# A mixture-of-experts layer whose last stage is folded into the expert blocks: the second expert's block adds the first one's row, normalises and writes the output

## The reference

```python
h = rmsnorm(x, norm_pre_ffn) * (1.0 + sc2) + sh2         # x: stream after token mixing
grp = argmax(h @ w_rg + b_rg)                            # 1 group of 4
top_v, top_i = lax.top_k(le_sel, 2)                      # 2 experts of the 8 of that group
w_top = softmax(top_v) * gate_g
def expert_block(args):                                  # 128 rows of one expert
    hid = silu(xb @ w_gate[e]) * (xb @ w_up[e])          # 1024 -> 512
    return hid @ w_down[e]                               # 512 -> 1024
out = sum over the two experts of a token of w_top * its row
x = x + g2 * rmsnorm(out, norm_post_ffn)                 # the result
```

## Time and profile before

| | us |
|---|---|
| runs | 2747.73, 2748.4, 2756.85 (median 2748.4) |
| span of the profiled execution | 2748.3 |
| own time of the profiled execution | not listed apart from its span |
| expert blocks, from the first instruction to PE's end | 1713 to 2640.9 |
| from the end of the last expert product to the end of the span | 107.4 |
| granted TensorE clock, mean | 0.924 of full speed |

### The profile page before, as it was taken

One profiled execution on the slowest core, in us unless ns is written; L12 is line 12 of the kernel. 1 busy time (PEld: TensorE's weight loads), 2 busy tenths in 40 slices (PEclk: granted clock), 3 DMA queues, 4 the chain that ended last, 5 costly groups with the idle time before them and its releaser, 6 DMA issues. The chain is left out here.

```text
span 2748.3 us, 36137 instructions
## 1 busy us (share of the span) xinstructions
PE 2291.0 (83%) x11720; PEld 1881.1 (68%) x11721; DVE 1460.6 (53%) x1901; ACT 1063.1 (39%) x1517; POOL 671.3 (24%) x743
## 2 busy tenths in 40 slices
PE   5899998999995626888867995799999999999940
PEld 2688887989983225666656884577777777787730
DVE  2333331111104865887864775286576656538857
ACT  2433333322221211433322222276566655537731
POOL 0000000000003345777731223222122212112322
PEclk8899999999996879999988996899999999999975
DMA  7222233121215868534435331498588868558968
GB/s 253 86 92 92 92 108 115 47 93 46 90 52 193 317 216 300 207 141 153 153 95 198 146 133 52 138 323 299 200 305 282 283 216 279 205 181 308 368 240 320
DMA packets 294684, 509.46 MB, mean 185 GB/s; under 512 B 35104, under 2 KB 209600, under 8 KB 290368
## 3 DMA queue, kind: packets, MB, share of 16 engines
q1 hardware_dynamic: 261200, 403.20, 42.4%
q0 software_dynamic: 21904, 63.54, 6.6%
q10 hardware_dynamic: 11520, 41.95, 3.8%
HBM read 408.16 MB, written 110.43 MB: 189 GB/s over the span
## 5 line engine op out<-in xcount | busy, mean ns | idle before, releaser
L2146 DVE TENSOR_TENSOR e_w_low<-e_w_whole,e_w_high 128x2048 fp32r<-128x2048 f32 x192 | 432.2, 2292 | 82.9 <-ACT e_w_high L2102 82.6
L2102 ACT ACTIVATE e_w_high<-e_w_whole 128x2048 fp32r<-128x2048 f32 x192 | 356.5, 1909 | 17.9 <-PEq L1491 12.3
L2056 PE MATMUL e_pG<-e_w_high,e_xT 128*128 128x512 f32 x768 | 305.0, 397 | 1.2 <-ACT e_xT L2095 1.2
L2057 PE MATMUL e_pG<-e_w_low,e_xT 128*128 128x512 f32 x768 | 305.3, 397 | 0.0
L611 PE MATMUL proj_acc<-w_high,hT_high 128*128 128x512 f32 x672 | 265.6, 395 | 6.9 <-DVE hT_low L646 5.7
L611 PE MATMUL proj_acc<-w_low,hT_high 128*128 128x512 f32 x672 | 263.0, 391 | 0.0
L611 PE MATMUL proj_acc<-w_high,hT_low 128*128 128x512 f32 x672 | 262.8, 391 | 0.0
L2075 PE MATMUL e_pY<-e_w_high,e_hT 128*128 128x512 f32 x768 | 221.7, 400 | 0.0
L2060 PE MATMUL e_pG<-e_w_high,e_xT 128*128 128x512 f32 x768 | 194.9, 395 | 0.0
L307 POOL TENSOR_TENSOR stat<-stat,eps 128x1 f32<-128x1 f32 x36 | 10.8, 300 | 725.0 <-ACT xn L515 725.0
L2056 PEld LDWEIGHTS e_pG<-e_w_high,e_xT 128*128 128x128 f32 x768 | 145.2, 189 | 36.6 <-issue 1.6
(11 more groups left out here) (287 smaller groups left out, 4403.3 us busy)
## 6 DMA issues: line engine op xcount, KB each, us to landing
e_w_whole<-in_moe_w_gate_dram SPq DMA_DIRECT2D x64, 1024.0 KB, 7.6
e_w_whole<-in_moe_w_up_dram SPq DMA_DIRECT2D x64, 1024.0 KB, 10.9
e_w_whole<-in_moe_w_down_dram SPq DMA_DIRECT2D x64, 1024.0 KB, 9.3
m_tok<-by_token SPq DMA_DIRECT2D x16, 1280.0 KB, 6.9
xt<-in_x_dram SPq DMA_DIRECT2D x32, 512.0 KB, 5.4
wm_rest<-in_w_mod_dram POOLq DMA_DIRECT2D x8, 2048.0 KB, 12.2
c_yy<-rows_done SPq DMA_DIRECT2D x32, 512.0 KB, 7.4
by_token<-tok SPq DMA_DIRECT2D x16, 768.0 KB, 5.6
```

The costliest lines, as they stand in the source:

```text
L2056: nc.tensor.matmul(pG[:, half], xT[:, 0, k], wh[:, half, w], start=(k == 0), stop=False)
L2057: nc.tensor.matmul(pG[:, half], xT[:, 0, k], wl[:, half, w], start=False, stop=False)
L2102: nc.scalar.activation(wh[:, third, part], raw[:, third, part], ACT.Copy).then_inc(whs.sem, 1)
L2146: nc.vector.tensor_tensor(wl[:, third, part], raw[:, third, part], wh[:, third, part].bitcast(F32), ALU.subtract).then_inc(wls.sem, 1)
```

## The change

There is no `combine`. The list entry of a row has five numbers in place of two: the token to gather; the row of a scratch tensor (now 2048 rows) if this expert is the token's first, that with the smaller number, or else a number out of range; the same token number if it is the second, or else out of range; the weight; and 1.0 or 0.0 for second or not. Out-of-range rows are skipped by the DMAs, padding rows too. In a block, DVE multiplies the hidden rows by the weight (as a scalar of the same instruction), then, at the end, adds the partner's row times the flag to the product (one instruction over 1024 columns from PSUM); ACT squares the sum; POOL scatters it to the first rows, makes the inverse root, and gathers the partner rows of the next block after that scatter has landed; DVE scales by the root and the modulation; in the next round POOL adds the residual rows, which it has gathered, scatters them to the output, and DVE hands the row numbers on through four small tiles. In `projection` POOL copies the input `x`, 8 MB, into the scratch tensor halfway, so that a skipped or stale row holds finite numbers.

```diff
@@ projection, POOL
-            with pool.Fori(0, 2 * NGR) as t:
...
+            roots(0, NGR)
+            pool.dma_start(dram["ys"], io["x"].rearrange("o t d -> (o t) d")).then_inc(ys_init.sem(0), 16)
+            roots(NGR, 2 * NGR)
+            pool.wait_ge(ys_init.sem(0), ys_init.at(0))
@@ residual, DVE: choose and place
+                V.tensor_tensor(fl[:, s, 0:1], fe[:, 0:1], fe[:, 1:2], ALU.is_lt)
+                link(V.tensor_tensor(fl[:, s, 1:2], fe[:, 1:2], fe[:, 0:1], ALU.is_lt))
...
-                link(V.reciprocal(g["wtop"][:, 0, r:r + 1], dn[:]))
-                link(V.tensor_tensor(g["wtop"][:, 1, r:r + 1], g["wtop"][:, 0, r:r + 1], ex[:, s], ALU.mult))
+                w0, w1 = (token[:, r, k, 3:4].bitcast(F32) for k in range(2))
+                link(V.reciprocal(w0, dn[:]))
+                link(V.tensor_tensor(w1, w0, ex[:, s], ALU.mult))
+                for k in range(2):
+                    V.scalar_tensor_tensor(out=to[:, k, 0:1], in0=fl[:, s, 1 - k:2 - k], scalar=float(SKIP), in1=row_f[:, r:r + 1], op0=ALU.mult, op1=ALU.add)
+                    m = V.scalar_tensor_tensor(out=to[:, k, 1:2], in0=fl[:, s, k:k + 1], scalar=float(SKIP), in1=row_f[:, r:r + 1], op0=ALU.mult, op1=ALU.add)
+                link(m)
+                link(V.tensor_copy(token[:, r, :, 1:3], to[:]))
+                for k in range(2):
+                    m = V.tensor_copy(token[:, r, k, 4:5].bitcast(F32), fl[:, s, 1 - k:2 - k])
+                link(m)
@@ experts, POOL
+            for at in (ids, held, first, second, done_row):
+                nc.gpsimd.memset(at[:], SKIP).then_inc(none.sem, 1)
+            for t in (xb[:], v[:], z, partner[:], x1):
+                nc.gpsimd.memset(t, 0.0).then_inc(none.sem, 1)
...
+            def load_ids(b, row):
+                pool.wait_ge(held_on.sem, held_on.at(b - 1))
+                pool.dma_start(ids[:], dram["ids"][bass.ds(row, P), :]).then_inc(ids_in.sem(0), 16)
+            def complete(b):
+                pool.wait_ge(x1_in.sem(0), b * 16 + 16)
+                pool.wait_ge(zs.sem, zs.at(b - 3))
+                nc.gpsimd.tensor_tensor(z, z, x1, ALU.add).then_inc(done.sem, 1)
+                pool.wait_ge(done.sem, done.at(b))
+                pool.indirect_dma_start(out_rows, rows(done_row, 0), z, None, bounds_check=SEQ - 1, oob_is_err=False).then_inc(out.sem(0), 16)
+            def gather_x1():
+                pool.indirect_dma_start(x1, None, x1_rows, rows(second, 0), ...).then_inc(x1_in.sem(0), 16)
+            def root(b):
+                pool.wait_ge(ssq.sem, ssq.at(b - 2))
+                nc.gpsimd.tensor_tensor(ss[:, 1:2], ss[:, 0:1], g["eps"][...], ALU.add).then_inc(eps_added.sem, 1)
+                nc.gpsimd.tensor_tensor(ss[:, 1:2], ss[:, 1:2], g["neghalf"][:, 0:1], ALU.pow).then_inc(rstd.sem, 1)
+            def hand_on(b):
+                pool.wait_ge(sums.sem, sums.at(b - 2))
+                pool.indirect_dma_start(dram["ys"], rows(first, 0), v[:], None, ...).then_inc(first_out.sem(0), 16)
+                root(b)
+                pool.wait_ge(first_out.sem(0), first_out.at(b))
+                pool.wait_ge(second_on.sem, second_on.at(b - 1))
+                pool.indirect_dma_start(partner[:], None, dram["ys"], rows(second, 0), ...).then_inc(partner_in.sem(0), 16)
+            def load(b, row, following):
+                load_ids(b, row)
+                complete(b)
+                gather_x1()
+                pool.wait_ge(ids_in.sem(0), ids_in.at(b))
+                gather_x(b)
+                hand_on(b)
@@ experts, ACT
-                act.wait_ge(y_out.sem(0), b * 16 + 48)
-                nc.scalar.activation(y[:, 0:512], pY[:, 0], ACT.Copy).then_inc(ya.sem, 1)
                 if following is not None:
                     high(following, 2)
+                act.wait_ge(sums.sem, sums.at(b))
+                nc.scalar.activation(sq, v[:], ACT.Square, accum_out=ss[:, 0:1]).then_inc(ssq.sem, 1)
@@ experts, DVE
+                    nc.vector.scalar_tensor_tensor(out=hid[...], in0=sg[:, half], scalar=held[:, 3:4].bitcast(F32), in1=pG[:, half, 1], op0=ALU.mult, op1=ALU.mult).then_inc(hids.sem, 1)
...
+                dve.wait_ge(first_out.sem(0), first_out.at(b + 1))
+                nc.vector.tensor_copy(first[:], held[:, 1:2]).then_inc(first_on.sem, 1)
+                hold(b + 1)
...
                 dve.wait_ge(prodY.sem, prodY.at(b))
-                nc.vector.tensor_copy(y[:, 512:D], pY[:, 1]).then_inc(yd.sem, 1)
+                dve.wait_ge(partner_in.sem(0), partner_in.at(b + 1))
+                dve.wait_ge(second_on.sem, second_on.at(b))
+                nc.vector.scalar_tensor_tensor(out=v[:], in0=partner[:], scalar=second[:, 2:3].bitcast(F32), in1=pY[...], op0=ALU.mult, op1=ALU.add).then_inc(sums.sem, 1)
                 if following is not None:
                     low(following, 2)
+                dve.wait_ge(rstd.sem, rstd.at(b + 2))
+                dve.wait_ge(out.sem(0), out.at(b + 2))
+                nc.vector.tensor_copy(done_row[:], second[:, 0:1]).then_inc(done_on.sem, 1)
+                nc.vector.scalar_tensor_tensor(out=z, in0=v[:], scalar=ss[:, 1:2], in1=g["mod"][:, 3], op0=ALU.mult, op1=ALU.mult).then_inc(zs.sem, 1)
+                take_second(b + 1)
...
-def combine(nc, kit, io, g, dram):
...
-    for stage in (modulation, projection, convolution, states, mixing, residual, experts, combine):
+    for stage in (modulation, projection, convolution, states, mixing, residual, experts):
```

225 lines of the change are left out of this document (96 added, 129 removed).

## The result

The changed kernel takes 2802.7 us (median of 4 runs, 2792.1 to 2807.6) against 2748.1 before: ratio 1.0188, 95% interval 1.0168 to 1.0207. It is slower by 1.9%, where 2713 us and a gain were forecast.

What follows compares the result with a forecast made beforehand. DVE's chain was taken to bound the 17 splitting blocks behind splitting ones, with PE's work setting the others. 2748.3 - 94 + 49 + 3 + 3 + 2 + 2 = 2713 us; own range 2690 to 2734, over all 2672 to 2758.

Steps and rivals of the forecast that it cites:

- the 17 blocks: Expert blocks that split the next expert's weights right behind another that splits: period 18.87 to 21.8 us, +49 in all.
- POOL's addition: Residual addition in the 17: 1.9 us on POOL, overlapping DVE's `low` and lengthening it by 1.5, bounds 0 to 1.9.
- The sum, scaling and copies: DVE at a splitting block's end: sum in place of the evacuation copy -0.34 us net, scaling and two small copies +1.7.
- DVE's wait for the root: At a splitting block's end DVE waits for POOL's root before scaling: 0.5 us taken, range 0 to 1.5.
- The other 31 blocks: Expert blocks outside the 17: added work ends inside DVE's 4.8 us wait for silu, so only +3 us in all.
- The loop through DRAM: Per-block circle of sum, scatter, landing, partner gather, landing: 18.7 us, POOL's round 17 to 27, 0 added to the time.
- The row of 2.80: A POOL DMA issue beside `low` taking 2.80 us, another 1.03; 2.80 throughout would make POOL's round 27 and cost 85.
- The loop closes (slower): Rival, chance 0.15: slow issues and landings make POOL's round set the 17 blocks' period; 2828 us in full, half 2748 to 2770.
- The Trainium skill's rule: A DVE `tensor_tensor` should not slow POOL's descriptor generation; POOL's round would stay at 17 us, adding 0.
- the copy of 8 MB: POOL's copy in `projection`: over before the weight loads, or queued with them if slower; +2 us, range 0 to 15.
- Tail: What remains after the last product, from sum to the output's landing and program end: 13 us in place of 107.4.
- DMA as the bound: Rival without a stated chance: 0.18 MB more moved per block, 0.5 us in the 17, hidden beside DVE's 2.9.

Runs made afterwards that it cites:

- experiment 2: Changed kernel with POOL's addition of the residual rows done in one column of 1024 only, so the output is wrong: 2744.8 us, ratio 0.998.
- experiment 1: Changed kernel with the inverse root taken off POOL's list, VectorE adding eps only, so the output is scaled wrongly: 2780.6 us, ratio 1.0108.
- experiment 13: Changed kernel with VectorE's `low` in instructions of 1024 elements in place of 2048, nothing else: 2747.6 us, ratio 0.9988.
- experiment 4: Kernel before the change with only the 8 MB copy into the scratch tensor added in `projection`: 2748.8 us, ratio 0.9998.
- best variant: Changed kernel, residual addition on VectorE, root wait and scaling behind the next block's first `e_hid`, `low` in 1024 elements: 2709.3 us, ratio 0.9856.

## Why the prediction was wrong

The profiled time is 93 us over the forecast: 75 in the expert blocks, 12 ahead of them, 6 in the tail.

- **What bounds the kernel.** The reading of the earlier trace rows was right: in the 17 blocks DVE's chain sets the time, before the change. Wrong was that it would after it. What bound the changed kernel in these 17 is POOL's round, of an engine at 22% in the expert blocks before.
- **POOL's addition.** Clash 1.37 for 1.5 forecast, right. In POOL's list it stood with 1.9 in a round that was put at 0 us of the period; it took 2.42 + 0.93 there, and with it gone the time fell by 58 us (experiment 2).
- **The sum, scaling and copies.** Right within 0.3. The 0.65 us at the turn of the loop was missing: work at the end of a list uncovers it.
- **DVE's wait for the root: 0.5 forecast, 2.0 measured.** "0 to 1.5 by the root's place behind POOL's issue of up to 2.8" counted one issue. There are four ahead of it, each 1.9 to 3.1 us. ACT's square was in time. Where such a block comes alone, opening the root's circle took it from 23.60 to 21.89 (experiment 1).
- **The other 31 blocks: +3 forecast, +50 measured.** This is the step that failed most. The argument was that the scaling ends 6 us into the next block, inside the wait for silu. It ends 8.3 us after the sum began, since the root waits for POOL, and the copy of the first rows' numbers waits for a landing ahead of PE's down product. With shorter issues alone (experiment 13) 14 of them fell from 20.88 to 19.18. The forecast also took the clock to stay as it was; about 7 of the 50 us stand beside its fall.
- **The loop through DRAM: 0 forecast.** Here both ends stood, 17 and 27 us of POOL's round, and the low one was chosen "since in the trace most issues are near 1.0". The round was 22.8 to 23.6. The count behind that choice was right (62 of the 93 took less than 1.05 us) and its reason was not looked for. About the same share of the issues began in a `low` before as after (54 of 93, 149 of 239), but before, 21 of the 54 began at the very start of one and were not held, and the other 33 took 1.69 us in the mean. After the change only one of the 149 began so, and the mean was 2.20 in `low` and 1.76 over all 239. The row of 2.80 was the rule and the row of 1.03 the exception. The rival *The loop closes (slower)*, chance 0.15, is what happened in kind: its period to decide was 23.8 us and the measured one 23.5, with 1.3 to 2.0 us in the others for the 1 that it had. Its landings of 8 to 9 us came (7.7 for the first rows, median); its ground that DMA is full did not, and its full round of 27 us did not either.
- **The Trainium skill's rule.** The Trainium skill (SBUF — State Buffer, section "Who interferes with whom") infers that descriptor generation is not slowed by a `tensor_tensor`. The measurement decides against that inference: 1.03 us beside an idle DVE, 2.20 beside `low`, and 55 us for `low` in shorter pieces. Another rule of the same section of the Trainium skill, that a DVE instruction with at most one SBUF input, outside its two-port modes, does not contend with GpSimd, agrees: 1.05 and 1.06 us beside the sum and `e_xT`.
- **The rest.** `residual` 4.0 for 3; start of the experts 4.5 for 2; the copy of 8 MB, forecast at 2, is free when alone (experiment 4), and the 5 us at the end of `projection` are within scatter. Tail 18.8 for 13: the hand-over to its own DMA and the 9.2 us from the last issue to the end. DMA as the bound: it was not; its share fell to 0.90 in the period.

What stays open: how much of the long periods with a fallen clock is the clock's own, and why some issues stand through many instructions of 512 elements.

## What to carry to other kernels

Before moving work onto an engine that nobody waits for, write out its list for one turn, in order, with every wait and every hand-over, and close the circle: from the event that starts the list to the instruction that the first engine needs back. Take issue times from rows where the other engine is doing what it will be doing then, not from the mean, and where two such rows differ (1.03 and 2.80), find out why before choosing one: the trace of before had the answer. And where POOL's indirect DMAs are in the circle, the length of VectorE instructions with two SBUF operands is a knob: 1024 elements in place of 2048 gave 55 us in the changed kernel and 31 in its best variant, and 512 in place of 1024 lost 73 there, about half of it beside a fallen clock. Compare periods at the same granted clock before putting them down to a wait.

## What the runs showed of the hardware

- An indirect DMA that POOL begins to issue while a VectorE instruction of two SBUF operands runs ended 0.8 to 1.0 us after the end of that instruction: 2.20 us in the mean beside `low` of 2048 elements in place of 1.03 beside an idle VectorE. Exceptions: those that began together with it (21 in the kernel before, 1.02 us), and those that stood to the end of the pair (3 of 149 with 2048 elements, 41 of 140 with 512).
- Beside VectorE instructions with one operand in PSUM it took 1.05 and 1.06 us.
- The granted TensorE clock in the expert blocks was 1.00 while PE was busy for 18.43 of 18.87 us a period, and 0.96 in the changed kernel, with PE busy for 18.55 of 23.58.
- The POOL addition of 128x1024 fp32 took 2.42 us here, for 1.90 in the earlier trace rows, and 0.93 passed before the DMA that reads its result was issued.
- A load of 2.5 KB landed 5.7 us (median) after its issue.
